# The first block's output projection as three fp32r products instead of one fp32 product

## The reference, cut to what matters

```python
y = (jax.nn.sigmoid(gate_sb + b_gate[0]) * (o_sb @ w_branch_sb)
     + jax.nn.sigmoid(gate_gla + b_gate[1]) * (o_gla @ w_branch_gla))
return y @ w_out            # [256, 1024] @ [1024, 1024], this is the product
...
h = h + mixing_sublayer(rms_norm(h, norm_mix_g[i]), ...)
hn = rms_norm(h, norm_ffn_g[i])
h = h + conv_ffn(hn, w_ffn_in[i], conv_w[i], conv_b[i], w_ffn_out[i])
```

## Time and profile before

| | us |
|---|---|
| median of 3 runs | 1500.98 |
| lowest and highest | 1499.5, 1501.61 |
| the profiled execution | 1502.64 |
| its span, first to last instruction | 1500.8 |
| PE busy in it | 1424.4 |
| DVE, POOL, ACT busy | 648.0, 407.2, 245.3 |

### The profile page before, as it was taken

How to read it: one execution, slowest core, us unless ns; L and a number is a source line. 1 busy time by engine, 2 the same in 40 slices (tenths; PEclk the granted TensorE clock), 3 DMA queues, 4 the chain that set the end, 5 groups by cost and what they waited for, 6 DMA issues and landing times.

```text
span 1500.8 us, 20320 instructions
## 1 busy us (share of the span) xinstructions
PE 1424.4 (95%) x7328; PEld 781.7 (52%) x7329; DVE 648.0 (43%) x1094; ACT 245.3 (16%) x422; POOL 407.2 (27%) x430
## 2 busy tenths in 40 slices
PE   8999999999989999999899999999899999999995
PEld 7768876999976664334334343343334333333332
DVE  2034744766754444333443344343434434333233
ACT  1122113444422320001001010010000000100001
POOL 3000001322216014343533434443543444200000
PEclk9999999999999999999999999999999999999998
DMA  7343334555443948999996999999999999999995
GB/s 259 128 140 141 112 113 145 181 179 196 152 153 134 353 176 351 429 428 428 427 428 277 430 428 427 427 428 428 428 427 428 428 428 427 428 429 429 427 427 212
DMA packets 77413, 480.73 MB, mean 320 GB/s; under 512 B 7019, under 2 KB 31272, under 8 KB 52808
## 3 DMA queue, kind: packets, MB, share of 16 engines
q1 hardware_dynamic: 74046, 477.45, 78.2%
q10 hardware_dynamic: 3338, 2.88, 0.6%
HBM read 479.26 MB, written 1.05 MB: 320 GB/s over the span
## 4 chain that ended last, share of the span: by engine, by line
PE 49%; DMA 40%; POOL 4%; DVE 3%; issue 2%; ACT 1%; POOLq 1%; SPq 0%; DVEq 0%; ACTq 0%
DMA stage<-in_w_gate_up 30%; PE bank L2072 9%; PE bank L1592 9%; PE bank L1826 8%; DMA ring<-in_w_gate_up 7%; PE bank L1602 7%; PE bank L2148 5%; PE bank L1838 4%; POOL ring L593 4%; PE bank L1758 2%; DMA ring_b<-in_w_gate_up 2%; DMA ring_b<-in_w_down 2%; PE bank L2053 1%; PE bank L2107 1%; POOLq L586 0%
## 5 line engine op out<-in xcount | busy, mean ns | idle before, releaser
L593 POOL COPY ring<-stage 128x1024 f32<-128x1024 f32 x300 | 309.4, 1077 | 446.2 <-DMA stage<-in_w_gate_up 360.5
L2072 PE MATMUL bank<-ring,x_T 128*64 128x512 f32 x1584 | 369.8, 613 | 37.6 <-POOL ring L593 30.1
L2072 PEld LDWEIGHTS bank<-ring,x_T 128*64 128x64 f32 x1584 | 111.4, 140 | 273.4 <-issue 206.4
L2148 PE MATMUL bank<-ring_b,act_T 128*64 128x512 f32 x1056 | 237.5, 600 | 1.0 <-ACT act_T L860 0.5
L1472 DVE TENSOR_TENSOR h<-h,bank 128x512 f32<-128x512 f32 x128 | 82.2, 684 | 244.3 <-PE bank L2107 244.3
L2148 PEld LDWEIGHTS bank<-ring_b,act_T 128*64 128x64 f32 x1056 | 72.5, 137 | 148.8 <-issue 127.9
L2072 PE MATMUL bank<-ring_b,x_T 128*64 128x512 f32 x528 | 120.6, 598 | 2.3 <-DMA ring_b<-in_w_gate_up 2.3
L1592 PE MATMUL bank<-x_nT,ring 128*128 128x256 f32 x512 | 114.9, 387 | 2.6 <-issue 2.6
L1448 DVE SCALAR_TENSOR_TENSOR y_lo<-bank,slot_gate,y_hi 128x512 fp32r<-128x512 f32 x33 | 24.8, 751 | 196.6 <-ACT y_hi L840 196.6
L1592 PEld LDWEIGHTS bank<-x_nT,ring 128*128 128x128 f32 x512 | 98.9, 194 | 17.3 <-issue 3.5
L854 ACT ACTIVATE sig<-bias_raw 128x512 f32<-128x512 f32 x33 | 20.8, 629 | 509.2 <-DVE bias_raw L1478 509.2
(11 more groups left out here) (426 smaller groups left out, 1562.8 us busy)
## 6 DMA issues: line engine op xcount, KB each, us to landing
stage<-in_w_gate_up SPq DMA_DIRECT2D x75, 2048.0 KB, 25.0
ring_b<-in_w_down SPq DMA_DIRECT2D x64, 2048.0 KB, 22.9
ring_b<-in_w_gate_up SPq DMA_DIRECT2D x32, 2048.0 KB, 21.0
ring<-in_w_gate_up SPq DMA_DIRECT2D x21, 2048.0 KB, 25.5
ring<-in_w_in SPq DMA_DIRECT2D x22, 1024.0 KB, 7.3
ring<-in_w_ffn_in SPq DMA_DIRECT2D x22, 1024.0 KB, 5.1
ring<-in_w_ffn_out SPq DMA_DIRECT2D x11, 1024.0 KB, 4.9
ring<-in_w_out SPq DMA_DIRECT2D x8, 1024.0 KB, 6.2
```

What stands on the lines that cost most here:

```text
L593: ins = pool.tensor_copy(pair_slot(g, pair)[:, cols], t.stage[:, pair, cols])
L2072: ins = pe.matmul(banks[n][rows, :], t.x_T[:, c, :], job_slot(g, c)[:, c0:c0 + 512], start=False, stop=(c == GU - 1), skip_group_check=True)
L2148: ins = pe.matmul(banks[4][rows, :], t.act_T[:, k, SLOTS * (c // 2):SLOTS * (c // 2) + SLOTS], job_slot(g, GU + c)[:, c0:c0 + 512], start= ...
```

## The change

The product `y @ w_out` becomes three fp32r products: rounded y by rounded w, rounded y by the rest of w, and the rest of y by rounded w, all into the same bank. ACT makes the rounded copies of the four weight chunks (`out_high`) and of the eight parts of y (`y_high_T`), in a hand-written order. POOL subtracts to make the rests of the weights, in place in the ring (`ring_r` lies over `ring`). DVE subtracts to make the rests of y (`y_low_T`), one part late in its loop, in place over `y_T`. The rounded copies lie in SBUF that earlier steps no longer use; for this, buffers are merged and put in another order.

```diff
     rsqrt("gla")
+    for i in range(4):
+        pool.wait_ge(s.out_rounded, i + 1)
+        raw = t.ring[:, slot_use(W_OUT + i)[0], :]
+        pool.tensor_tensor(t.ring_r[:, slot_use(W_OUT + i)[0], :], raw, t.out_hi[i][:].bitcast(F32), ALU.subtract).then_inc(s.out_split, 1)
...
+    def out_high(i):
+
+        slot, value = slot_use(W_OUT + i)
+        act.wait_ge(s.landed[slot], value)
+        act.activation(t.out_hi[i][:], t.ring[:, slot, :], ACT.Copy).then_inc(s.out_rounded, 1)
+
+    def y_high_T(f):
+
+        act.wait_ge(s.y_ready, f + 1)
+        act.activation(t.y_hi_T[:, f, :], t.y_T[:, f, :], ACT.Copy).then_inc(s.y_rounded, 1)
+
+    act.wait_ge(*r1.filled("gate7"))
+    for i in range(2):
+        out_high(i)
+    for f in range(5):
+        y_high_T(f)
+    out_high(2)
+    y_high_T(5)
+    out_high(3)
+    for f in range(6, KT):
+        y_high_T(f)
...
+    def y_low_T(f):
+
+        dve.wait_ge(s.y_rounded, f + 1)
+        dve.tensor_tensor(t.y_lo_T[:, f, :], t.y_T[:, f, :], t.y_hi_T[:, f, :].bitcast(F32),
+                          ALU.subtract).then_inc(s.y_split, 1)
+
     for f in range(KT):
...
         dve.tensor_tensor(t.y_T[:, f, :], y_a, y_b, ALU.add).then_inc(s.y_ready, 1)
+        if f > 0:
+            y_low_T(f - 1)
+    y_low_T(KT - 1)
...
-    wo = w_in(24)
-    for b in range(NB):
-        project(r1, f"wo0{b}", b, wo, t.y_T, 0, 512, ready=y_ready)
-    wo = w_in(26)
-    project(r1, "wo10", 0, wo, t.y_T, 0, 512)
+    def mixed_out(n, b):
+
+        bank = open_bank(r1, f"wo{n}{b}")
+        for k in range(KT):
+            i = 2 * n + k // 4
+            cols = slice(512 * (k % 4), 512 * (k % 4) + 512)
+            if b == 0 and k % 4 == 0:
+                pe.wait_ge(s.out_rounded, i + 1)
+                pe.wait_ge(s.out_split, i + 1)
+            if n == 0 and b == 0:
+                pe.wait_ge(s.y_rounded, k + 1)
+                pe.wait_ge(s.y_split, k + 1)
+            w_hi, w_lo = t.out_hi[i][:, cols], t.ring_r[:, slot_use(W_OUT + i)[0], cols]
+            y_hi, y_lo = (m[:, k, b * P:(b + 1) * P] for m in (t.y_hi_T, t.y_lo_T))
+            pe.matmul(bank[:], y_hi, w_hi, start=(k == 0), stop=False)
+            pe.matmul(bank[:], y_hi, w_lo, start=False, stop=False)
+            ins = pe.matmul(bank[:], y_lo, w_hi, start=False, stop=(k == KT - 1))
+        ins.then_inc(s.filled, 1)
+
+    for b in range(NB):
+        mixed_out(0, b)
+    mixed_out(1, 0)
...
-    project(r1, "wo11", 1, wo, t.y_T, 0, 512)
+    mixed_out(1, 1)
```

More of the change, by code:

```diff
@@ L58 @@
 RING = 6
+W_OUT = 24
 CW = 2048
@@ L232, in build @@
         t = Buffers()
+        with ExitStack() as stack:
+            t.rounded(into(stack))
         t.persistent(into(ctx))
-        for phase in (t.mixer, t.ffn, t.attention, t.experts):
+        for phase in (t.mixer, t.mixed, t.ffn, t.attention, t.experts):
             with ExitStack() as stack:
@@ L691, in scalar_program @@
     act.wait_ge(s.gla_cum, 1)
-    act.activation(t.dec_q[:], t.cum[:], ACT.Exp, scale=-1.0 / 16).then_inc(s.gla_exp, 1)
-    act.activation(t.dec_k[:], t.cum[:], ACT.Exp, scale=1.0 / 16).then_inc(s.gla_exp, 1)
-    act.activation(t.dec_e[:], t.cum_end[:], ACT.Exp, scale=1.0 / 16).then_inc(s.gla_exp, 1)
+    act.activation(t.dec_q, t.cum[:], ACT.Exp, scale=-1.0 / 16).then_inc(s.gla_exp, 1)
+    act.activation(t.dec_k, t.cum[:], ACT.Exp, scale=1.0 / 16).then_inc(s.gla_exp, 1)
+    act.activation(t.dec_e, t.cum_end[:], ACT.Exp, scale=1.0 / 16).then_inc(s.gla_exp, 1)
     for n in range(4):
@@ L697, in scalar_program @@
     weights_of_half(1)
-    take(r1, "kend", t.k_end[:], r1.bank("kend")[:].rearrange("p (b n) -> p b n", b=NB))
+    take(r1, "kend", t.k_end, r1.bank("kend")[:].rearrange("p (b n) -> p b n", b=NB))
     for n in range(2):
@@ L1056, in vector_program @@
         step(dve.tensor_copy(t.chunk_decay[:, k, :], t.dec_q[:, k, CH - 1:T:CH]))
-    dve.tensor_tensor(t.dec_q[:], t.g_q[:], t.dec_q[:], ALU.mult).then_inc(s.gla_dec, 1)
-    dve.tensor_tensor(t.dec_k[:], t.g_k[:], t.dec_k[:], ALU.mult).then_inc(s.gla_dec, 1)
-    dve.tensor_tensor(t.dec_e[:], t.g_k[:], t.dec_e[:], ALU.mult).then_inc(s.gla_dec, 1)
+    dve.tensor_tensor(t.dec_q, t.g_q[:], t.dec_q, ALU.mult).then_inc(s.gla_dec, 1)
+    dve.tensor_tensor(t.dec_k, t.g_k[:], t.dec_k, ALU.mult).then_inc(s.gla_dec, 1)
+    dve.tensor_tensor(t.dec_e, t.g_k[:], t.dec_e, ALU.mult).then_inc(s.gla_dec, 1)
     arguments_of(1)
@@ L1781, in tensor_program @@
             branch(f, q)
-    def y_ready(k):
-        pe.wait_ge(s.y_ready, k + 1)
-    wo = w_in(24)
+    def mixed_out(n, b):
[15 more added lines that the diff above has]
+        ins.then_inc(s.filled, 1)
     for b in range(NB):
-        project(r1, f"wo0{b}", b, wo, t.y_T, 0, 512, ready=y_ready)
-    wo = w_in(26)
-    project(r1, "wo10", 0, wo, t.y_T, 0, 512)
+        mixed_out(0, b)
+    mixed_out(1, 0)
     for b in range(NB):
@@ L2271, in __init__ @@
         self.y_ready = new("y_ready")
+        self.y_rounded = new("y_rounded")
+        self.y_split = new("y_split")
+        self.out_rounded = new("out_rounded")
+        self.out_split = new("out_split")
         self.ff_zero = new("ff_zero")
@@ L2363, with rounded, mixed @@
 class Buffers:
+    def rounded(self, new):
+        self.ring_r = new("ring_r", [RING, CW], F32R)
+        self.y_lo_T = new("y_lo_T", [KT, T], F32R)
+    def mixed(self, new):
+        new("under_x_nT", [1184])
+        out_hi = [new("out_hi0", [CW], F32R), new("out_hi3", [CW], F32R)]
+        new("under_z", [1024])
+        out_hi.insert(1, new("out_hi1", [CW], F32R))
+        new("z_end", [1024])
+        out_hi.insert(2, new("out_hi2", [CW], F32R))
+        self.out_hi = out_hi
+        new("under_dec", [11520])
+        self.y_hi_T = new("y_hi_T", [KT, T], F32R)
     def persistent(self, new):
+        self.ring = new("ring", [RING, CW])
+        self.x_n = new("x_n", [NB, D])
         self.h = new("h", [NB, D])
-        self.x_n = new("x_n", [NB, D])
-        self.ring = new("ring", [RING, CW])
         self.ident = new("ident", [P])
@@ L2414, in mixer @@
         self.x_nT = new("x_nT", [KT, T])
-        self.sb_q = new("sb_q", [4, T])
-        self.sb_k = new("sb_k", [4, T])
+        self.sb_qk = new("sb_qk", [8, T])
+        self.sb_q, self.sb_k = self.sb_qk[:, 0:4, :], self.sb_qk[:, 4:8, :]
         self.sb_v = new("sb_v", [NB, 512])
@@ L2433, in mixer @@
         self.cum_end = new("cum_end", [2, T])
-        self.dec_q = new("dec_q", [2, T])
-        self.dec_k = new("dec_k", [2, T])
-        self.dec_e = new("dec_e", [2, T])
+        self.dec = new("dec", [8, T])
+        self.dec_q, self.dec_k = self.dec[:, 0:2, :], self.dec[:, 2:4, :]
+        self.dec_e, self.k_end = self.dec[:, 4:6, :], self.dec[:, 6:8, :]
         self.chunk_decay = new("chunk_decay", [2, 4])
-        self.k_end = new("k_end", [NB, KW])
         self.att = new("att", [8, P])
```

## The result

The changed kernel takes 1503.76 us in the median of 20 runs, the one before 1502.26 us in 20 runs. The medians are 1.5 us apart; the ratio over all the runs is 1.0017, 95% interval 1.0009 to 1.0024: 2.5 us slower (1.4 to 3.6). The forecast was 0.9 us slower. The profiled execution has a span of 1501.3 us against 1500.8.

The account below looks back on a forecast made before the run. PE alone was taken to bound the kernel from 190.06 to 232.26 us. Products -5.2, first stall +3.75 and second stall +2.3 made +0.9 us: median 1500.98 to 1501.9, range 1495.5 to 1506.

Parts of the forecast that it names:

- the two meetings: POOL's weight subtractions hold up DVE operations with two SBUF operands, at 188 and at y6: +3.75 and +2.3 us.
- rival A: Clock falls to half when PE restarts at 193.8; branches 3.1 us later, sum +4.0, 1505.0 us; chance 0.22.
- three products for one: Output projection on PE: 96 fp32r matmuls at 0.232 us replace 64 fp32 records taking 27.5 us; saves 5.2 us.
- first stall: PE stands before the transposes, starting them at 193.8 instead of 190.06, because DVE's scaling waits for POOL: +3.75 us.
- second stall: PE waits in `wo00` for parts 5 and 6 of y, 1.1 and 1.15 us: +2.3 us.
- the cover given for ACT: ACT was idle from 183.60 to 216.96, so its added roundings were to cost nothing.
- The first meeting: At 188, POOL's first subtraction leads DVE's attention scaling by 0.15 us; scaling takes about 5.5 instead of 1.23.
- rival B: DVE starts first at 188: no first stall, second stall 3.4 us, sum -1.8, 1499.2 us; chance 0.18.
- The second meeting: At y6, POOL's third and fourth subtractions delay DVE's addition of `y6` (about 2.5 us) and `y_low_T(5)` (4.8).
- One DVE operation per boundary: Between back-to-back POOL instructions one DVE operation passes, then POOL has it again; so `y_low_T(5)` ends at 220.1.
- Rival C: In-place writes or short operations pass POOL, so all is hidden and -5.2 us stands: 1495.8 us; chance 0.13.
- D: Projection products miss 0.232 us because weights change with each matmul: about +6 us, 1507 us; chance 0.05.

Follow-up runs that it names:

- almost no subtraction: Changed kernel with POOL subtracting 16 of a chunk's 2048 columns and the second product taking rounded weights instead of their rests; stretch 51.90 us, ratio to before 0.9957.
- busy PE with late pieces: Changed kernel with 15 spare matmuls before PE's wait for scaled attention output, and POOL's third and fourth subtractions in eight pieces; stretch 55.75 us, ratio 0.9986.
- late pieces: Changed kernel with only POOL's third and fourth subtractions cut into eight pieces; stretch 57.42 us, ratio to before 0.9993.
- the run with the old products: Changed kernel with PE making the fp32 products of before, roundings and subtractions kept but rests unused; stretch 63.92 us, ratio to before 1.0046.
- the second run of the eight pieces: Repeat of the changed kernel with each of POOL's four subtractions cut into eight of 256 columns; stretch 51.95 us, ratio to before 0.9943.
- the first experiment: Changed kernel with POOL's first subtraction waiting until DVE has scaled the attention output; stretch 56.28 us, ratio to before 1.0001.
- the busy PE: Changed kernel with 15 spare matmuls on PE just ahead of its wait for the scaled attention output; stretch 59.62 us, ratio to before 1.0012.

## Why the prediction was right, and where not

The time fell inside the range and the two meetings came as worked out, but the forecast's sum was 1.5 us short: it put the clock at nothing, and the clock fell. That is neither the case it called most likely (0.42, both stalls and the clock kept) nor rival A with its 3.1 us.

The runs split the 2.39 us by differences of stretches between before, almost no subtraction, busy PE with late pieces, late pieces, and the changed kernel. Such a chain adds up to 2.39 by construction, so the sum tests nothing; what tests a term is its reading in the trace of the changed kernel, in the last column. The readings of the three losses add up to 7.50 us, against 7.64 by the differences.

| term | predicted | measured | from | read in the changed kernel |
|---|---|---|---|---|
| three products for one | -5.2 | -5.25 | almost no subtraction - before | 0.232 from start to start, as predicted |
| first stall | +3.75 | +3.85 | busy PE with late pieces - almost no subtraction | 3.74, transposes' start against before |
| clock after the first stall | 0, or +3.1 as rival A | +1.67 | late pieces - busy PE with late pieces | 1.65, lost by transposes and next branch |
| second stall | +2.3 | +2.12 | changed kernel - late pieces | 2.11, from starts (below) |
| sum | +0.9 | +2.39 | | |

*The bound.* PE alone set the end of this stretch, and a microsecond here was one at the end: 6.8 and 6.9 us in the run with the old products, 2.39 and 2.5 in the changed kernel. Of the kernels with a ratio only the second run of the eight pieces has an interval that leaves its stretch out.

*The products.* 0.232 us from start to start held, and the cover given for ACT, for the FFN's first chunk and for SP held too.

*The first meeting.* Order, lead (0.15 predicted, 0.14 measured), length of the scaling (5.5 and 5.45) and idle PE (3.7 and 3.59) were as worked out. The inference from nearly simultaneous starts to a lead for POOL carried; rival B, which had DVE win, was what the first experiment made real. B's sum was -1.8; that stretch came out 0.87 under before, because its second stall was 0.8 shorter than B's 3.4 and the clock, which B leaves out too, took 1.7.

*The second meeting.* One DVE operation per boundary, inferred from the experts' copies, put 2.5 us on the addition of `y6` and 4.8 on `y_low_T(5)`; they took 2.20 and 4.81. PE restarted at 220.39 and 221.98, predicted were 220.1 and 221.95. That the times within the span agree so well is partly luck: the stretch began 1.24 us earlier than before, and the clock's 1.65, which the forecast left out, came on top. It was close elsewhere too: `y_low_T(4)` ended at 210.61, 0.07 us ahead of POOL's third subtraction. The profile's idle times of 1.11 and 0.66 count from modelled ends of matmuls; from start to start (218.88 to 220.39, 220.92 to 221.98, each less 0.232) the waits are 1.28 and 0.83, together 2.11, against 1.1 and 1.15.

*The clock.* This is the term that failed. The forecast took the clock as kept, and gave the case that it falls 0.22. It fell, and the sign that the prediction named for rival A, a clock under 1.00 after 194, came: 0.58 in 194 to 196. Rival A in turn was mis-sized: it took 6.3 us at half clock from the kernel's start (its rows give 5.9, from 14.92 to about 20.85), and 3.3 us of work at half clock followed here, from 192.4 to about 195.7. So its 1505.0 came from a restart that was slow for longer than this one. The truth lay between the forecast and rival A. Rival A also put the deciding stall above 2.31 us; the runs have falls behind shorter ones (last section), so its condition was wrong as well. Rival C (no lock) and D (slow products) fell with the measured lengths.

What the trace of before could not tell, the runs showed: whether the clock falls is not decided by the length of one gap alone. It fell at the first stall or behind the second, though never at both in the profiled executions. Gaps of 1.11 and 0.66 us in the changed kernel left it up, and 1.18 and 0.66 with the busy PE were followed by a fall. What makes the difference stays open, and there is one trace for each kernel: how often other executions fall isn't known.

## What to carry to other kernels

Before giving POOL work beside DVE, list which DVE operations in that time have two SBUF operands and which of them lie on the path; each may wait for one whole POOL instruction. The cure is not to move the work but to cut it: in pieces of 256 columns the same subtractions cost POOL 30% more time and PE nothing, and turned 2.5 us lost into 5.2 gained. A stall on PE should be priced with a fall of the clock behind it, and taking away one of two stalls may only move that fall to the other: here it did so twice.

## What the runs showed of the hardware that was not expected

The clock fell after short gaps too. With a first stall of 3.59 us it fell there, and the later gaps of 1.11 and 0.66 left it at 1.00. With the first stall removed or filled, gaps of 1.66 and 0.64, or 1.18 and 0.66, were followed by some 3.4 us at 0.5. Before, a single gap of 2.31 did not the earlier trace rows. The Trainium skill, TensorE: Matmul & The Clock Gate, section HAM oscillation, speaks of idle gaps between bursts; that a gap can be followed by the lower level is what the trace shows too, with the 3.59 us. Its section A second HAM failure mode: psum-queue depth-cycling adds that in one kernel short idle times between groups of matmuls were frequent enough to make the clock go back and forth between its levels. No run here shows that: there are two short gaps and one fall in each execution.

The fall doesn't always begin in the gap. In the changed kernel the clock was down when PE restarted at 192.40. With the late pieces PE restarted at 193.53 at full clock, and it fell only at about 194.65, when PE had been busy for a microsecond; it cost 1.67 us. The run with the old products did the same (restart 193.74, fall 195.05), and behind the second stall the two falls came 0.5 and 0.2 us after the restart. So a full clock at the restart doesn't mean that the stall was free.
